# The rwkv stage of a two block kernel: low rank mixes a tile ahead, the first tiles of decay and keys two units up, and the first batch of block inversions on VectorE instead of GpSimd

## The reference, cut to what matters

```python
xx = token_shift(h) - h
xr, xw, xk, xv, xa, xg = (h + xx * mu[i] for i in range(6))
r, k, v = xr @ w_r, xk @ w_k, xv @ w_v                 # each 1024 x 1024
w = -softplus(-(w0 + tanh(xw @ w1) @ w2)) - 0.5        # low rank, 64 wide
a = sigmoid(a0 + (xa @ a1) @ a2)                       # low rank, 64 wide
g = sigmoid(xg @ g1) @ g2                              # low rank, 160 wide
kk = normalised(k * k_k);  k = k * (1 + (a - 1) * k_a);  decay = exp(-exp(w))
# 16 heads of 64, state S, token by token:
S_t = S_{t-1} diag(decay_t) + (S_{t-1} (-kk_t)) (kk_t a_t)^T + v_t k_t^T
y_t = S_t r_t
```

## Time and profile before

| | us |
|---|---|
| median of three runs | 3236.98 (3236.17 to 3237.77) |
| the profiled execution, own time | 3237.95 |
| its span in the profile | 3236.1 |
| TensorE busy in the span | 2901.8 (90%) |
| VectorE busy | 1573.0 (49%) |
| ScalarE busy | 1000.3 (31%) |
| GpSimd busy | 666.3 (21%) |

### The profile page before, as it was taken

The page is one execution under the profiler, slowest core; times in us unless marked ns, Lnnn a source line. Parts: engine busy times, 40 slices in busy tenths (PEclk is TensorE's granted clock), DMA queues, the critical chain, the costliest instruction groups (busy, mean ns, idle before and its releaser), DMA issues. The chain is left out here.

```text
span 3236.1 us, 38094 instructions
## 1 busy us (share of the span) xinstructions
PE 2901.8 (90%) x13928; PEld 2294.1 (71%) x13928; DVE 1573.0 (49%) x1974; ACT 1000.3 (31%) x1522; POOL 666.3 (21%) x634
## 2 busy tenths in 40 slices
PE   6799999679889879999889877689999987999999
PEld 4678888335788758888668765368888763688887
DVE  3377762523643467774333465455443336663432
ACT  3333332114321133332223243343222233732221
POOL 0021111312540123111100052352111201431100
PEclk9899999789988879999899878789999998999999
DMA  3222233211100003223223200113233320022233
GB/s 126 65 71 93 97 93 95 68 33 46 59 8 1 9 20 98 97 95 89 83 73 97 59 1 1 43 34 100 97 97 91 98 85 1 1 94 95 97 91 104
DMA packets 79430, 218.81 MB, mean 68 GB/s; under 512 B 21805, under 2 KB 21933, under 8 KB 78798
## 3 DMA queue, kind: packets, MB, share of 16 engines
q1 hardware_dynamic: 78878, 213.29, 21.4%
q10 hardware_dynamic: 432, 3.90, 0.3%
HBM read 215.06 MB, written 2.10 MB: 67 GB/s over the span
## 5 line engine op out<-in xcount | busy, mean ns | idle before, releaser
L281 PE MATMUL psum<-rounded,high_r 128*128 128x512 f32 x3040 | 1200.2, 395 | 65.3 <-DVE rounded L246 41.0
L283 PE MATMUL psum<-rounded,high_r 128*128 128x512 f32 x3040 | 1189.8, 391 | 0.0
L285 PE MATMUL psum<-rounded,ring_low 128*128 128x512 f32 x3040 | 1189.3, 391 | 0.0
L301 ACT ACTIVATE high_r<-ring 128x1024 fp32r<-128x1024 f32 (+2 forms) x432 | 420.2, 973 | 1540.7 <-PE psum L285 1501.2
L306 DVE TENSOR_TENSOR ring_low<-ring,high_r 128x1024 fp32r<-128x1024 f32 (+2 forms) x432 | 520.4, 1205 | 757.7 <-ACT high_r L301 756.4
L281 PEld LDWEIGHTS psum<-rounded,high_r 128*128 128x128 f32 x3040 | 574.6, 189 | 210.2 <-issue 56.7
L283 PEld LDWEIGHTS psum<-rounded,high_r 128*128 128x128 f32 x3040 | 575.5, 189 | 119.6 <-issue 2.6
L285 PEld LDWEIGHTS psum<-rounded,ring_low 128*128 128x128 f32 x3040 | 574.9, 189 | 120.5
L658 DVE TENSOR_TENSOR arena<-psum,inverse 128x512 f32<-128x512 f32 x176 | 121.5, 691 | 315.2 <-PE psum L285 315.0
L558 POOL CAST rounded<-rows 128x512 f32 (+1 forms) x88 | 53.8, 611 | 784.8 <-DVE rows L663 784.8
L1705 POOL TENSOR_SCALAR arena<-arena,small 128x512 f32<-128x512 f32 x64 | 99.6, 1564 | 196.8 <-DVE small L1674 196.0
(11 more groups left out here) (302 smaller groups left out, 3004.5 us busy)
## 6 DMA issues: line engine op xcount, KB each, us to landing
ring<-in_up SPq DMA_DIRECT2D x176, 512.0 KB, 3.3
ring<-in_down SPq DMA_DIRECT2D x64, 384.0 KB, 3.1
ring<-in_down SPq DMA_DIRECT2D x64, 320.0 KB, 2.9
ring<-in_even_in SPq DMA_DIRECT2D x36, 512.0 KB, 3.6
ring<-in_sgu_in SPq DMA_DIRECT2D x16, 512.0 KB, 3.4
ring<-in_even_out SPq DMA_DIRECT2D x16, 384.0 KB, 3.1
ring<-in_qkv SPq DMA_DIRECT2D x12, 512.0 KB, 3.6
ring<-in_sgu_out SPq DMA_DIRECT2D x8, 512.0 KB, 3.3
```

The lines of the kernel that those rows point to most:

```text
L281: nc.tensor.matmul(psum[:, m, :], high_r[:, r % HIGHS, blk], x_high, start=(k0 + k == 0), stop=False)
L283: nc.tensor.matmul(psum[:, m, :], high_r[:, r % HIGHS, blk], x_low, start=False, stop=False)
L285: mm = nc.tensor.matmul(psum[:, m, :], ring_low[:, r % R, blk], x_high, start=False, stop=end)
L301: nc.scalar.activation(high_r[:, r % HIGHS, 0:nk * P], ring[:, r % R, 0:nk * P], ACT.Copy).then_inc(unit_high, 1)
```

## The change

Four things are done in the rwkv mixer.

1. VectorE mixes the low rank inputs of tile 0 before the key stream, and those of tile n + 1 after the other two mixes of unit n, instead of those of tile n ahead of them. The wait for the three tiles to be read (`low_rank_used`) moves along; the wait for the low rank weights stays on TensorE alone.
2. Rates and in-rates come four pairs each after receptance units 0 and 1. `spread_and_sum(0..3)`, the powers and the hats follow units 2 to 5, the first pairs of diagonal scores units 6 and 7, `spread_and_sum(4..7)` value units 0 to 3, and the other pairs value units 4 and 5. The first unit's scores follow value unit 6, in PSUM banks 4 to 7.
3. The first batch of blocks is inverted by VectorE, in pieces of 3, 3, 9, 9 and 7 steps after the work of value units 2 to 6. Behind the last piece VectorE turns the second batch in, masks the first unit's scores and turns the first batch back. GpSimd inverts the second batch alone.
4. Tiles are laid out anew to allow this, the clearing of the state and of one tile of solved blocks moves to VectorE behind the value stream, and ScalarE's spread of the first unit stands ahead of its copies of the second half of the values.

```diff
 def kept(u, kind):
-    return heads(XN + 6 if kind == N else XN + 3 * (u % 2) + kind - 1)
-carried = [heads(XN + 7), heads(XX + 7)]
-solved = [heads(XX + b) for b in range(2)]
+    return heads(XX + 3 if kind == N else (XX, XN)[u % 2] + kind - 1)
+carried = [heads(XN + 3 + b) for b in range(2)]
+solved = [shrink[:, :].rearrange("p (h t) -> p h t", h=4), heads(XN + 5)]
...
+def score_bank(u, step):
+    return 2 * step if u else 4 + 2 * step
...
-def substitute(pool, b, steps):
-
-    for n, t in enumerate(range(BLOCK - 1, 0, -1)):
+def substitute(eng, ops, b, steps, lo=0, hi=BLOCK - 1):
+
+    for n in range(lo, hi):
+        t = BLOCK - 1 - n
         w = BLOCK - t
         part = square_sum[:, 0:t * w].rearrange("p (s w) -> p s w", w=w)
-        pool.wait_ge(steps, 2 * n + 2)
-        nc.gpsimd.tensor_tensor(part, lower[b][:, 0:t, t:t + 1].to_broadcast([P, t, w]),
+        eng.wait_ge(steps, 2 * n + 2)
+        ops.tensor_tensor(part, lower[b][:, 0:t, t:t + 1].to_broadcast([P, t, w]),
                                 inv[b][:, t:t + 1, t:BLOCK].to_broadcast([P, t, w]), ALU.mult).then_inc(steps, 1)
-        pool.wait_ge(steps, 2 * n + 3)
-        nc.gpsimd.tensor_tensor(inv[b][:, 0:t, t:BLOCK], inv[b][:, 0:t, t:BLOCK], part, ALU.add).then_inc(steps, 1)
+        eng.wait_ge(steps, 2 * n + 3)
+        ops.tensor_tensor(inv[b][:, 0:t, t:BLOCK], inv[b][:, 0:t, t:BLOCK], part, ALU.add).then_inc(steps, 1)
...
+        def score(u, step):
+            if u == 0:
+                pe.wait_ge(diagonal_kept, 8 * BLOCKS)
+            elif u == 1:
+                pe.wait_ge(v_taken, 8)
+            else:
+                pe.wait_ge(masked, 4 * (u - 1) + 2 * step + 2)
+            for w, kind in enumerate(((N, RB), (AK, RK))[step]):
+                for j in range(4):
+                    i, e = divmod(j, 2)
+                    lhs, rhs = score_operands(u, j, kind)
+                    at = (2 * w + i) * P
+                    mm = nc.tensor.matmul(psum[:, score_bank(u, step) + e, at:at + P], lhs, rhs, start=True, stop=True)
+            mm.then_inc(scored, 1)
+
         def with_r(n):
             if n == 0:
                 gather(KD - 1)
-            if n < 4:
-                for m in (2 * n, 2 * n + 1):
+            if n < 2:
+                for m in range(4 * n, 4 * n + 4):
                     rate(m)
                     in_rate(m)
+            elif n < 6:
+                spread_and_sum(n - 2)
             else:
-                spread_and_sum(n - 4)
+                pair_of_units(2 * n - 12)
+                pair_of_units(2 * n - 11)
 
         def with_v(n):
-            if n in (0, 1):
-                pair_of_units(2 * n)
-                pair_of_units(2 * n + 1)
-            elif n in (6, 7):
-                pair_of_units(2 * n - 8)
-                pair_of_units(2 * n - 7)
-            else:
-                spread_and_sum(n + 2)
+            if n < 4:
+                spread_and_sum(n + 4)
+            elif n < 6:
+                pair_of_units(2 * n - 4)
+                pair_of_units(2 * n - 3)
+            elif n == 6:
+                score(0, 0)
+                score(0, 1)
...
-            pe.wait_ge(masked, 4 * u + 1)
+            pe.wait_ge(masked, 4 * u + 1 if u else 2)
...
+            else:
+                pe.wait_ge(v_taken, 8)
...
-        score(0, 0)
-        score(0, 1)
-        pe.wait_ge(diagonal_kept, 8 * BLOCKS)
         carry(0)
...
-            if n < 4:
-                for j in (2 * n, 2 * n + 1):
+            if n < 2:
+                for j in range(4 * n, 4 * n + 4):
                     act.wait_ge(rates_done, j + 1)
                     nc.scalar.activation(rates[:, j // 2, j % 2 * T:(j % 2 + 1) * T], psum[:, 4 + j % 2, :],
                                          ACT.Sigmoid).then_inc(rates_kept, 1)
                     act.wait_ge(a_done, j + 1)
                     nc.scalar.activation(tile(AA + j), psum[:, 6 + j % 2, :], ACT.Sigmoid, bias=col("a0", j)).then_inc(a_kept, 1)
+            elif n < 6:
+                raise_powers(n - 2)
             else:
-                raise_powers(n - 4)
+                keep_diagonal(2 * n - 12)
+                keep_diagonal(2 * n - 11)
...
-        def after_v(g, m, done):
-            n = 4 * g + m
-            if n in (0, 1):
-                keep_diagonal(2 * n)
-                keep_diagonal(2 * n + 1)
-            elif n in (6, 7):
-                keep_diagonal(2 * n - 8)
-                keep_diagonal(2 * n - 7)
-            else:
-                raise_powers(n + 2)
...
+            if u < 2:
+                act.wait_ge(cleared, 2 * u + 1)
...
+        def after_v(g, m, done):
+            n = 4 * g + m
+            if n < 4:
+                raise_powers(n + 4)
+            elif n < 6:
+                keep_diagonal(2 * n - 4)
+                keep_diagonal(2 * n - 3)
+            elif n == 6:
+                spread(0)
+        split_and_read(act, "rwkv_k", split_high, after_k)
...
-        act.wait_ge(cleared, 3)
-        spread(0)
...
-        def during_k(g, m, done):
-            n = 4 * g + m
-            if n == 0:
-                dve.wait_ge(lw1_loaded, 16)
-            else:
+        def low_rank_mix(n):
+            if n:
                 dve.wait_ge(low_rank_used, n)
             for which, to in zip((1, 4, 5), low_rank_in):
                 mix(which, n, to).then_inc(low_rank_mixed, 1)
+
+        def during_k(g, m, done):
+            n = 4 * g + m
             mix(0, n, tile(WW + n)).then_inc(r_mixed, 1)
             mix(3, n, tile(XN + n)).then_inc(v_mixed, 1)
+            if n + 1 < KD:
+                low_rank_mix(n + 1)
+        low_rank_mix(0)
...
-            if n >= 4:
-                dve.wait_ge(r_taken, n - 3)
-                hats(n - 4)
-
-        def during_v(g, m, done):
-            n = 4 * g + m
-            if n == 1:
-                dve.wait_ge(diagonal_kept, 4 * BLOCKS)
-                turn_in(0).then_inc(turned_in, 1)
             if 2 <= n < 6:
-                dve.wait_ge(r_taken, n + 3)
-                hats(n + 2)
-        split_and_read(dve, "rwkv_k", split_low, during_k)
-        split_and_read(dve, "rwkv_r", split_low, during_r)
-        split_and_read(dve, "rwkv_v", split_low, during_v)
-        dve.wait_ge(diagonal_kept, 8 * BLOCKS)
-        turn_in(1).then_inc(turned_in, 1)
-        dve.wait_ge(steps0, SUBSTITUTED)
-        turn_back(0).then_inc(turned_back, 1)
+                dve.wait_ge(r_taken, n - 1)
+                hats(n - 2)
...
+            bank = score_bank(u, n // 2)
...
+        def during_v(g, m, done):
+            n = 4 * g + m
+            if n == 0:
+                dve.wait_ge(r_taken, KD)
+                dve.wait_ge(diagonal_kept, 4 * BLOCKS)
+                turn_in(0).then_inc(turned_in, 1)
+            if n < 4:
+                hats(n + 4)
+            if 2 <= n < 7:
+                substitute(dve, nc.vector, 0, steps0, *((0, 3), (3, 6), (6, 15), (15, 24), (24, 31))[n - 2])
+            if n == 6:
+                dve.wait_ge(diagonal_kept, 8 * BLOCKS)
+                turn_in(1).then_inc(turned_in, 1)
+                for k in range(4):
+                    mask(0, k)
+                dve.wait_ge(steps0, SUBSTITUTED)
+                turn_back(0).then_inc(turned_back, 1)
...
-        dve.wait_ge(cleared, 3)
-        for n in range(4):
-            mask(0, n)
+        dve.wait_ge(unit_done, v_end)
+        dve.wait_ge(cleared, 1)
+        nc.vector.memset(state, 0.0).then_inc(cleared, 1)
+        nc.vector.memset(solved[1], 0.0).then_inc(cleared, 1)
...
-        pool.wait_ge(turned_in, 1)
-        substitute(pool, 0, steps0)
-        pool.wait_ge(unit_done, v_end)
-        nc.gpsimd.memset(state, 0.0).then_inc(cleared, 1)
-        pool.wait_ge(summed, KD)
-        for x in solved:
-            nc.gpsimd.memset(x, 0.0).then_inc(cleared, 1)
         pool.wait_ge(hats_done, KD)
+        nc.gpsimd.memset(solved[0], 0.0).then_inc(cleared, 1)
         identity(pool, 1, steps1)
         pool.wait_ge(turned_in, 2)
-        substitute(pool, 1, steps1)
+        pool.wait_ge(steps0, SUBSTITUTED)
+        substitute(pool, nc.gpsimd, 1, steps1)
```

More of the change, by code:

```diff
@@ L777, in kept @@
             def kept(u, kind):
-                return heads(XN + 6 if kind == N else XN + 3 * (u % 2) + kind - 1)
-            carried = [heads(XN + 7), heads(XX + 7)]
-            solved = [heads(XX + b) for b in range(2)]
+                return heads(XX + 3 if kind == N else (XX, XN)[u % 2] + kind - 1)
+            carried = [heads(XN + 3 + b) for b in range(2)]
+            solved = [shrink[:, :].rearrange("p (h t) -> p h t", h=4), heads(XN + 5)]
             def squares_of_blocks(x):
                 return x.rearrange("p (a b) -> p a b", b=BLOCK)
-            diagonal = [squares_of_blocks(flat(rows[:, 0:2, :])), squares_of_blocks(span(XX + 2, 2))]
-            lower = [squares_of_blocks(span(WW, 2)), squares_of_blocks(span(XX + 4, 2))]
```

(34 more changed lines are left out.)

## The result

The changed kernel takes 3183.99 us (median of four runs, 3183.5 to 3185.16), the kernel before, beside it on the same chip, 3236.61 us (four runs). The ratio is 0.9837, with a 95% interval of 0.982 to 0.9854: 52.6 us faster. The forecast was 3178, range 3163 to 3196, so the gain is 6 us short of the 58.6 forecast.

A forecast was written before the change was run, and what follows sets the result against it. In the key stream TensorE waits 4.45 us in each of eight units for VectorE's low rank mixes, which also costs clock. Terms -57.2 - 1.9 + 0.5 = -58.6 us take 3236.98 to 3178, range 3163 to 3196.

The forecast's parts named there:

- Term 1: Key stream: mixing low rank inputs one tile ahead saves 57.2 us, 35 of idle time and 22 of clock.
- Rates, -9.8 + 3: Receptance stream: first spread 9.8 us earlier with rates in two units; 3 us lost to clock after a 1.4 us wait.
- End of the value stream, +4.9: First spread to carry: VectorE's inversion sets the end, 114.1 us instead of 109.2, so 4.9 us later.
- the line that the prediction drew through 128 and 512: VectorE's inversion: an operation costs 0.15 us plus 1.03 ns an element, from operations of 128 and 512 elements.
- Rival B: End of value stream: inversion on VectorE is dear, 37.6 us, +14, total 3192; chance 0.15.
- The chunk units are unchanged.: Recurrence behind the carry: its time was forecast to stay the same, a term of nothing.
- Rival C: Cheap inversion, no clock cost from the 1.4 us wait, or the chunk units' low clock not recurring: 3165 to 3172; chance 0.2.
- Rival A: Key stream: low rank products stay at 1.2 GHz though idle goes; saving 35 us, total 3200; chance 0.07.
- D: Key stream and first two receptance units: clock never rises from half, slower, 3262 us; chance 0.02.
- E: Key stream: the new order does nothing, TensorE waiting for a weight load or split instead, 3232 us; chance 0.01.

The follow-up runs named there:

- fill_keys: The kernel before with five products on constants, results unread, in each of the key stream's eight 4.45 us waits: 3220.86 us, ratio 0.9947.
- rates_two_six: The changed kernel with two pairs of rates after receptance unit 0 and six after unit 1, not four and four: 3179.01 us, ratio 0.982.
- fill_carry: The changed kernel with the four masks ahead of the inversion's last piece and nine unread products in TensorE's wait ahead of the carry: 3177.63 us, ratio 0.9808.
- fill_three: The changed kernel with the four masks ahead of the inversion's last piece and three unread products in the wait ahead of the carry: 3183.24 us, ratio 0.983.
- gpsimd_first: The changed kernel with the first batch inverted by GpSimd right behind its turn in, no pieces on VectorE: 3178.19 us, ratio 0.9817.
- rest_only: The changed kernel with the key stream's low rank mixes back in their old order: 3242.72 us, ratio 1.0017 to the kernel before.
- gpsimd_two_six: The changed kernel with the first batch inverted by GpSimd and the rates two and six pairs: 3177.32 us, ratio 0.9797.
- fill_unit5: The changed kernel with four extra products of 256 columns in TensorE's 1.7 us wait in recurrence unit 5: 3177.19 us, ratio 0.98.
- gpsimd_two_six_fill5: The changed kernel with GpSimd inverting the first batch, rates two and six, and four extra products in unit 5's wait: 3156.22 us, ratio 0.9756.
- masks_first: The changed kernel with only the first unit's four masks moved ahead of the inversion's last piece: 3184.18 us, ratio 0.9829.

## Why the prediction was right, and where it was off

**Term 1, -57.2 us: right in both parts.** The receptance product was forecast at 690.1 and started at 689.56, 57.8 us earlier than before. The period of the unit is 9.58 us where 9.70 was forecast, but that is in part luck: the eight slots come to 632.08 - 628.47 = 3.61 us, not 4.11, and the product to 5.97, not 5.59, two errors of opposite sign. The start was 0.7 us later than thought. VectorE's mixes were forecast too cheap as well: the five take 4.79 us, not 3.4 (1013 ns each over the key stream), and end 7.2 us after the unit's end, not 5.8. GpSimd's split of the mix of r runs beside them, but no run separates the two. The next low rank group wants them at 9.6, so it cost nothing. The split into 35 of idle time and 22 of clock is shown by `fill_keys`, whose carry moved by 22.9 with the idle time left in place as work. Nor did the new wait on the input tiles and the split queued behind it cost anything.

**Rates, -9.8 + 3: right.** The third rate waited 1.19 us (1.4 forecast) and the clock fell; `rates_two_six` prices both at 4.7 (4.4 forecast). That the clock would fall was a guess between two rows, and the right one. The first spread came 64.1 us earlier, 57.2 + 9.8 - 3 = 64.0 by the forecast; in parts it is 57.8 + 6.3 for 57.2 + 6.8.

**End of the value stream, +4.9: right.** From first spread to carry 842.41 - 728.59 = 113.8 us, forecast 114.1; idle ahead of the carry 8.14, forecast 8. The inversion's pieces took 1.5, 1.95, 7.6 and, the last two together, 12.0 us: 23.05, forecast 23.1. The two operations shown above, 31 elements in 0.20 us and 256 in 0.42, lie within 0.02 us of the line that the prediction drew through 128 and 512. The estimate from the Trainium skill (VectorE: DVE Perf Modes, the DRAIN section and the 1x cycle account) was 21.6 us. The trace nearly agrees: the 62 operations are busy for 21.2 us, and the other 1.9 us lie between dependent operations. Rival B is false. The hats held 0.68 us. No product of the value stream waited for a split.

**What failed: "The chunk units are unchanged."** They issue the same work and took 6.2 us more, which is the 6 us by which the gain fell short. At full clock they aren't dearer: `fill_carry` ran all of them in 184.6 us, nearly all of it at full clock. They spent 48 us near half clock in place of 39: the fall behind the carry took 32 us, not 15.6, and the second one was shorter than before. By the granted clock 5.8 of the 6.2 us were lost to it. Rival C had the right mechanism, but only in the direction of a gain: it allowed that the low stretch might not recur when the work ahead shifts, not that one might grow. A stretch whose clock isn't at full before the change is a term with two signs, and I put one of them at nothing. The prediction had named the chunk units getting longer as a sign of being wrong, and that sign came.

**The rest.** Rival A is refuted by `fill_keys` too, D and E by the clock and waits of the key stream. Of C, the inversion was not cheap and the third rate's wait did cost clock. My later guess, that the length of the wait ahead of the carry sets the length of the fall, fell with `fill_three`.

**Still open** is what decides how long the clock stays low in the first chunk units. The carry has stood behind 0.4, 5.4, 5.8 and 8.1 us of wait, and in the three kernels with the inversion on GpSimd behind none that the trace shows. 15 to 32 us of half clock followed in all traces but `gpsimd_first`'s (some 10 us) and `fill_carry`'s (none). The same wait of 5.8 us was followed by 15.6 us at half clock in the kernel before and by 29 in `fill_keys`. Runs of one and the same kernel differ by 8 to 13 us. That it is the clock is shown; what tips it is not, and so a gain of under some 10 us in this stretch can't be put down to an edit with the runs made here.

## What to carry to other kernels

Price a short wait of TensorE by what comes behind it as well: here 4.45 us of waiting made the next group of products 2.7 us dearer in every unit, 1.2 us cost another 3.5, and 1.7 us another 7 in the changed kernel. It is no fixed price: in `fill_carry` a wait of the same 1.7 us was followed by full clock. The test is cheap and needs no new schedule. Put products whose results nobody reads in the place of the wait, and see what becomes of the work behind them: what part of the gain would be the clock's is then known by itself. Take several runs of it, as one trace shows one of its levels only. When several edits come together, time each alone; here one of them held all of the gain, and the others, priced rightly at next to nothing on the path up to the carry, cost 5 us by themselves, with a recurrence 4.8 us longer whose amount of work they left as it was.

## What the runs showed that I had not expected

The clock fell again within the recurrence without a wait over 0.61 us. TensorE in the changed kernel:

```profile
858.00:862.00 4.00, 3.39 (x20) 0.67 0.00 0
862.00:866.00 4.00, 4.00 (x30) 0.75 0.00 0
866.00:870.00 4.00, 4.00 (x26) 0.50 0.00 0
...
874.00:878.00 4.00, 4.00 (x22) 0.54 0.00 0
878.00:882.00 4.00, 3.44 (x32) 1.00 0.00 0
```

It rises at 858, is back at half by 866 although TensorE is busy in all of that slice and the next, and comes to full only from 878. In the key stream, whose products have 512 columns, a wait of 4.45 us was made good within 8 us; behind the carry, among products of 64 and 128 columns, the low clock lasted 15.6 us in the kernel before and 29 in `fill_keys`, both after 5.8 us of wait, and 32 in the changed kernel.

Five traces (`rest_only`, `rates_two_six`, `fill_keys`, `gpsimd_first`, `gpsimd_two_six`) have a third, short fall some 40 us behind the start of the second, within 3 us of a wait of only 0.61 us, and the one fall of `fill_carry` before 1020 follows the same wait. `gpsimd_two_six_fill5` has it too, at 956.76, and stays at full clock.

Four kernels (`fill_carry`, `fill_unit5`, `gpsimd_two_six`, `gpsimd_two_six_fill5`) had runs at two levels, 8 to 13 us apart, with the program and the chip the same; `masks_first` had one run of five 8 us below the rest.
